# Conformer convolution, sample block, last layer norm and the hand-over of the second half of the tokens, in a four-layer decoder trunk

## The reference, cut to what matters

```python
hp = xp * (1 + sc1p) + sh1p                       # the same for the samples, per sample sequence
op = gmlp_mixer | conv_module | mla (hp)
xp = layer_norm(ALPHA * xp + g1p * op, ln_mix_g[i], ln_mix_b[i])
fp = swiglu_ffn(xp * (1 + sc2p) + sh2p, ffn_w_gate[i], ffn_w_up[i], ffn_w_down[i])
xp = layer_norm(ALPHA * xp + g2p * fp, ln_ffn_g[i], ln_ffn_b[i])

def conv_module(h, ctx, ...):
    a = h @ w_pw1 + b_pw1
    a = a[..., :D_MODEL] * jax.nn.sigmoid(a[..., D_MODEL:])
    full = jnp.concatenate([ctx, a], 1)
    y = depthwise(full, w_dw) + b_dw              # 31 taps along the tokens
    y = jax.nn.silu(layer_norm(y, ln_g, ln_b))
    return y @ w_pw2 + b_pw2, full[:, -(CONV_WIDTH - 1):]

# gmlp_mixer:  z = gelu(h @ w_in);  u, v = halves of z;  v = layer_norm(v);  y = (u * spatial(v)) @ w_out
```

## Time and profile before

| what | before |
|---|---|
| median of 3 executions | 3214.94 us (3214.44 to 3221.95) |
| the profiled execution's own time | 3222.54 us |
| its span, first to last instruction | 3220.3 us |
| PE busy | 3064.5 us, 95% |
| DVE, POOL, ACT busy | 46%, 47%, 17% |
| mean granted clock of PE | 0.983 |

### The profile page before, as it was taken

How to read it: one execution, slowest core, us unless ns; L and a number is a source line. 1 busy time by engine, 2 the same in 40 slices (tenths; PEclk the granted TensorE clock), 3 DMA queues, 4 the chain that set the end, 5 groups by cost and what they waited for, 6 DMA issues and landing times.

```text
span 3220.3 us, 54527 instructions
## 1 busy us (share of the span) xinstructions
PE 3064.5 (95%) x22828; PEld 2858.6 (89%) x22828; DVE 1485.7 (46%) x2487; ACT 543.7 (17%) x1114; POOL 1523.6 (47%) x904
## 2 busy tenths in 40 slices
PE   6999999999999799999999799999999999899997
PEld 5999989999876789999885488999989999899997
DVE  3254653324653753423656445342462535634346
ACT  3121130000220230000224103000022211400002
POOL 2355455545468445545420135554544464555551
PEclk8999999999999899999999999999999999999998
DMA  6542443443243243443222324333322322222221
GB/s 230 216 116 81 121 165 123 131 131 119 82 123 95 81 163 122 132 132 118 75 62 58 107 86 166 123 131 131 119 60 74 104 83 77 78 81 85 83 83 50
DMA packets 455970, 353.86 MB, mean 110 GB/s; under 512 B 26041, under 2 KB 437041, under 8 KB 443422
## 3 DMA queue, kind: packets, MB, share of 16 engines
q1 hardware_dynamic: 441232, 323.74, 31.8%
q10 hardware_dynamic: 14493, 26.63, 2.8%
HBM read 336.81 MB, written 5.25 MB: 106 GB/s over the span
## 4 chain that ended last, share of the span: by engine, by line
PE 81%; DVE 9%; ACT 3%; DVEq 2%; SPq 1%; issue 1%; DMA 1%; ACTq 1%; POOL 1%; POOLq 0%
PE pb L826 80%; DVE h_lo L2107 1%; ACT hf L1590 1%; DVEq L2055 1%; ACT h_hi L1590 1%; DVE pb L2073 1%; DVE part L2054 1%; DMA ada_first<-in_ada_w 1%; DVE xa L2080 1%; DVEq L2079 0%; DVE a_lo L1921 0%; SPq L700 0%; SPq L704 0%; SPq L702 0%; PE pb L921 0%
## 5 line engine op out<-in xcount | busy, mean ns | idle before, releaser
L733 POOL TENSOR_SCALAR w_hi<-w_raw 128x1024 fp32r<-128x1024 f32 (+2 forms) x416 | 448.5, 1078 | 1382.2 <-DMA w_raw<-in_ffn_w_up 400.8
L736 POOL TENSOR_TENSOR w_lo<-w_raw,w_hi 128x1024 fp32r<-128x1024 f32 (+2 forms) x416 | 986.3, 2371 | 69.0 <-issue 69.0
L826 PE MATMUL pb<-h_hi,w_hi 128*128 128x288 f32 x3584 | 975.6, 297 | 22.4 <-DVE h_lo L2107 15.9
L826 PE MATMUL pb<-h_lo,w_hi 128*128 128x288 f32 x3584 | 969.5, 296 | 0.0
L826 PEld LDWEIGHTS pb<-h_hi,w_hi 128*128 128x128 f32 x3584 | 676.1, 189 | 34.5 <-DVE h_lo L2107 21.5
L826 PEld LDWEIGHTS pb<-h_lo,w_hi 128*128 128x128 f32 x3584 | 676.9, 189 | 0.3
L826 PE MATMUL pb<-a_hi,w_hi 128*128 128x288 f32 x2176 | 594.1, 298 | 24.5 <-DVEq L2401 13.1
L826 PE MATMUL pb<-a_lo,w_hi 128*128 128x288 f32 x2176 | 588.6, 295 | 0.0
L826 PE MATMUL pb<-h_hi,w_lo 128*128 128x288 f32 x3584 | 556.4, 295 | 0.0
L826 PEld LDWEIGHTS pb<-h_hi,w_lo 128*128 128x128 f32 x3584 | 504.5, 188 | 0.0
L826 PEld LDWEIGHTS pb<-a_hi,w_hi 128*128 128x128 f32 x2176 | 409.7, 188 | 32.6 <-DVEq L2401 13.5
(11 more groups left out here) (283 smaller groups left out, 2729.5 us busy)
## 6 DMA issues: line engine op xcount, KB each, us to landing
ada_w<-in_ada_w SPq DMA_DIRECT2D x88, 1024.0 KB, 8.0
w_raw<-in_ffn_w_gate SPq DMA_DIRECT2D x88, 512.0 KB, 3.8
w_raw<-in_ffn_w_up SPq DMA_DIRECT2D x88, 512.0 KB, 3.7
w_raw<-in_gmlp_w_in SPq DMA_DIRECT2D x64, 512.0 KB, 4.4
w_raw<-in_ffn_w_down SPq DMA_DIRECT2D x64, 512.0 KB, 3.6
w_raw<-in_gmlp_w_out SPq DMA_DIRECT2D x32, 512.0 KB, 4.4
w_raw<-in_ffn_w_down SPq DMA_DIRECT2D x32, 384.0 KB, 3.3
w_raw<-in_conv_w_pw SPq DMA_DIRECT2D x24, 512.0 KB, 3.8
```

The source lines that it names most:

```text
L733: nc.gpsimd.tensor_scalar(w_hi[:, s, 0:w], w_raw[:, s, 0:w], 1.0, 1.0, ALU.mult, ALU.mult).then_inc(split_hi, 1)
L736: nc.gpsimd.tensor_tensor(w_lo[:, s, 0:w], w_raw[:, s, 0:w], w_hi[:, s, 0:w].bitcast(F32), ALU.subtract).then_inc(split_lo, 1)
L826: return nc.tensor.matmul(out, lhsT, rhs, start=start, stop=stop)
```

## The change

Four parts.

1. **Sample block.** The stationary block of the fifth token tile is `h_both`: 64 columns `h_lo` and 64 columns `h_hi` of the samples, side by side. Both pass under `w_hi` in one matmul and under `w_lo` in another, 16 matmuls for 24. The two parts then lie in different partitions of the bank and are added: ACT copies the lower one to `v_low`, DVE adds it, then comes the Gelu; in MLA, DVE does all of it. DVE builds `h_both` at the beginning of `gmlp` and `mla` (`sample_pairs`), and PE leaves this block to the last part of the second half.
2. **Second half by pairs.** `second_half(p)` hands over two channel tiles; DVE's order is now two `normalise`, `early`, and then per pair: samples, split, next `normalise`. PE takes the second half in four parts. `halves` of the first half stays at four tiles.
3. **Convolution.** The bias `gate * b_pw2` of the prompt goes into `ab`, the shift that ACT adds anyway, and POOL keeps the samples' share alone. `s_sum` and `s_sq` are added up by DVE. POOL makes `diag` for tile m + 1 behind its product for tile m. ACT writes the Silu twice (`hf` and `a_hi`), DVE only subtracts, by pairs, and PE takes the first half of `w_pw2` by pairs. PE transposes the states before the taps' weights.
4. **Last norm.** The channels of the last residual are transposed first, between the last products, into token-major tiles `yt`; the moments come from BN_STATS along the row, and gain and bias are added by POOL (`fgb`, loaded by SP) for the lower parts and by DVE for the upper parts. `second_stats`, the partition sums and the last `normalise` are gone for this norm; eight output transfers take the place of five.

```diff
+def token_parts(hi, lo, both, t):
+    if t == TT - 1:
+        return (lambda k: both[:, k, :],)
+    cols = slice(t * P, (t + 1) * P)
+    return lambda k: hi[:, k, cols], lambda k: lo[:, k, cols]
...
@@ pool, conv
                 for m in range(KT):
                     split_to(plan.mark[l, min(m + 2, KT - 1)])
                     if m == 0:
                         pool.wait_ge(w4_in, 16 * QT)
-                    if m >= 2:
-                        pool.wait_ge(taps_done, m - 1)
...
+                        diagonals(0)
                     pool.wait_ge(full_ready, m + 1)
...
-                    if m:
-                        pool.wait_ge(ysq_ready, m)
-                        pool.drain()
-                        for acc, y in ((s_sum, yc[:, m - 1, :]), (s_sq, sqy[:, (m - 1) % 2, :])):
-                            last = nc.gpsimd.tensor_tensor(acc[:], acc[:], y, ALU.add)
-                        last.then_inc(q_done, 1)
+                    if m + 1 < KT:
+                        if m:
+                            pool.wait_ge(taps_done, m)
+                        diagonals(m + 1)
                     if m == 3:
                         pool.wait_ge(xa_ready, 16 * (2 * l + 1))
...
-                        for k in range(KT):
-                            nc.gpsimd.tensor_scalar(xa[:, k, 0:SEQ], xa[:, k, 0:SEQ], gbw[:, k, 0:1], None, ALU.add)
...
@@ pe, first_four
-                for part_ in range(2):
-                    pe.wait_ge(h_ready, 4 * t + 2 * h + part_ + 1)
+                parts = 4 if h else 2
+                kn = KT // parts
+                for part_ in range(parts):
+                    if h and part_ % 2 == 0:
+                        pe.wait_ge(h_pair, 2 * t + part_ // 2 + 1)
+                    else:
+                        pe.wait_ge(h_ready, 4 * t + 2 * h + (part_ // 2 if h else part_) + 1)
...
@@ act, gmlp_v
+                if tt == TT - 1:
+                    fn(v_low[NS:], pb[0:NS, G.n % BANKS, 0:256], ACT.Copy).then_inc(low_copied, 1)
+                    act.wait_ge(low_added, LA.up())
...
@@ act, conv
+                act.wait_ge(bias_ready, 1)
                 residuals(2 * l)
...
+                        for dst in (hf[:, g, i, :], a_hi[:, m, half_cols(h)]):
+                            last = fn(dst, yc[:, m, half_cols(h)], ACT.Silu,
...
@@ dve, down_norm
+                second.normalise(0, 2)
+                second.normalise(2, 4)
+                early()
+                for p in range(4):
+                    samples(t, p)
+                    second_half(p)
+                    if p < 2:
+                        second.normalise(2 * p + 4, 2 * p + 6)
...
@@ dve, conv, taps
+                    if m:
+                        dve.wait_ge(ysq_ready, m)
+                        for acc, y in ((s_sum, yc[:, m - 1, :]), (s_sq, sqy[:, (m - 1) % 2, :])):
+                            last_ = v.tensor_tensor(acc[:], acc[:], y, ALU.add)
+                        last_.then_inc(q_done, 1)
...
@@ dve, conv, the end
+                def lower(h, p):
+                    ms = slice(2 * p, 2 * p + 2)
+                    dve.wait_ge(hfc_ready, 4 * h + p + 1)
+                    v.tensor_tensor(a_lo[:, ms, half_cols(h)], hf[:, p // 2, 2 * (p % 2):2 * (p % 2) + 2],
+                                    a_hi[:, ms, half_cols(h)].bitcast(F32), ALU.subtract)
+                    dve.drain().then_inc(a_ready, 2)
+
+                def pairs(stats, h):
+                    for p in range(4):
+                        stats.normalise(2 * p, 2 * p + 2, yc, yn_ready)
+                        if p:
+                            lower(h, p - 1)
+                    lower(h, 3)
...
@@ pool, behind the last split
+            for n, (tt, cols) in enumerate(((0, slice(0, D)), (1, slice(0, D)), (2, slice(0, 512)), (3, slice(0, 512)))):
+                pool.wait_ge(xh_ready, n + 1)
+                nc.gpsimd.tensor_tensor(yt[:, tt, cols], yt[:, tt, cols], fgb[:, 0, cols], ALU.mult)
+                pool.drain()
+                nc.gpsimd.tensor_tensor(yt[:, tt, cols], yt[:, tt, cols], fgb[:, 1, cols], ALU.add
+                                        ).then_inc(y_pool, 1)
```

446 lines of the change are left out of this document (297 added, 149 removed).

## The result

| | before | after |
|---|---|---|
| median of 4 executions | 3218.03 us (3214.44 to 3221.95) | 3181.90 us (3179.18 to 3183.53) |
| the profiled execution, its span | 3222.54 us, 3220.3 | 3183.53 us, 3181.7 |
| ratio, 95% interval | | 0.9884 (0.9871 to 0.9897) |
| mean granted clock of PE | 0.983 | 0.985 |

The change makes the kernel 36.1 us faster by the medians and 39.0 between the profiled executions. Forecast were 46.4 us and 3168.5 us: the direction is right and the time lies in the range, but the gain is 10.3 us too large (7.8 between the traces); 3.1 us more come from the median of before, which a fourth execution moved from 3214.94 to 3218.03.

The account below looks back on a forecast made before the run. PE, busy 95% of the span, was taken as the bound: its matmuls and its waits count. Terms 14.4 + 0.3 + 13.0 + 0 - 2.5 + 8.4 + 12.8 = 46.4 us, from 3214.9 to 3168.5 us; range 3153 to 3187.

Parts of the forecast that it names:

- first two rivals: Lock in the convolution and at the end: 3180 us, chance 0.13; waits move but the clock stays: 3178 us, chance 0.15.
- Part 1: Sample block, layers 0 and 3: eight fewer matmuls in each column group, 15 x 0.96 = 14.4 us less.
- Part 2: Sample block in MLA: between 0 and 1.9 us less, taken as 0.3 because PE waits behind it for DVE.
- Parts 3 and 4: Second half by pairs: 13.0 us less at t = 1, 2, 3, 5, 7; 0 at t = 4; -2.5 at t = 6.
- Part 5: Convolution: 6.4 + 3.0 + 1.4 - 2.4 = 8.4 us less.
- (a): Convolution: POOL's bias work goes, with PE's 3.03 us wait for w_hi and a 3.4 us slow stretch: 6.4 us less.
- (b): Convolution: diag of the last tile no longer waits for ACT's square and two additions; PE's 3.00 us wait goes.
- (e): Beginning of the convolution: DVE makes the bias first, and PE's short wait for transposes stays; no gain or loss charged.
- (c): Two norms at the convolution's end: a_lo and Silu by pairs, no cast, ACT writes twice; 1.4 us less.
- (d): Convolution: DVE takes 14 additions, four of them in the last two tiles held 0.6 us each by POOL's splits: -2.4.
- The first rival: Convolution and end: six DVE operations each wait a whole POOL operation of 2.4 us, 14 us; time 3180, chance 0.13.
- Part 6: Last norm: 31.2 us behind the last product become 18.4, with POOL the longest chain: 12.8 us less.

Follow-up runs that it names:

- e12: Changed kernel with the sample block of layers 0 and 3 made of three products again (24 matmuls, no h_both there): 3195.14 us.
- e9: Changed kernel with the second half at t = 0 alone handed over by four channel tiles, t = 1 to 7 still by pairs: 3181.11 us.
- e6: Changed kernel with the second half handed over by four channel tiles again at all eight inputs, no pairs: 3191.24 us.
- e1: Changed kernel with DVE making the convolution's bias behind its eight copies of the states instead of ahead of them: 3179.84 us.
- e8: Changed kernel with the convolution's bias made behind the first two tiles of full, and ACT's residual behind its third set of x4 transfers: 3180.49 us.
- e3: Changed kernel with POOL starting its five splits of w_pw2 only when the last yc is written, DVE's operations unchanged: 3177.57 us.
- e10: Changed kernel with DVE, in the last norm, inverting the deviations of token tiles 0 and 1 before adding product (6, second half): 3181.68 us.

## Why the forecast was right in direction, and where it was wrong

The range held the time, but 3181.90 us lies 13.4 from the forecast 3168.5 and nearer to the first two rivals, 3180 and 3178. Neither of them is what happened as a whole: the lock cost 5.4 us in the last two tiles and not 14, and the pairs kept most of their gain. The miss is mostly one part, the convolution (-6.6 us); elsewhere errors of both signs cancel.

**Part 1, 14.4 us: right.** e12 gives 13.2. Layer 0 shows only 5.8 of 7.7 us because part 3 takes 1.5 of it back there (e9).

**Part 2, 0.3: right.** PE's wait grew from 3.70 to 5.39 us while 1.92 us of matmuls went, 0.2 us net. No run tests it by itself, and the stretch as a whole holds a slow clock worth 2 us (last section).

**Parts 3 and 4, 10.5: about right in sum (9.3 by e6, 7.8 by its trace), wrong in two terms.** First, the step "t = 1, 2, 3, 5, 7" leaves out t = 0. PE has no wait for `h_lo` pairs there, but behind them the v statistics give its banks back, and the split costs 1.5 us (e9). The sentence that it "costs little here" and "the sum stays" was wrong at this place: the rule of the Trainium skill (VectorE: DVE Perf Modes, "Rules for kernel authors", minimise the number of operations) held where DVE has nothing but that work. Second, the clock. Two stretches of 1.7 us were taken as gone, since the earlier trace rows shows 0.52 behind a wait of 1.82. In e6 the same wait at three places is followed by a clock of 1.00. The slow stretch follows such a wait in some executions only (two of the six places: t = 1 and 3 before, not t = 5 before, none in e6), so 3.4 was an accident of one trace, not a price. At t = 7, where I took 1.1 us of it, the clock is 0.50 after as before. t = 6 cost 2 us less than I had priced, t = 5 brought 1.4 more. That the sum came out near 10.5 is luck in part: these two cover what t = 0 and the clock took.

**Part 5, 8.4 (8.9 with the second wait of t = 2): wrong, 2.3 measured.** Step by step: (a) the bias on POOL, 6.4, and (b) `diag`, 3.0, together 9.4, measured 8.8 between first and last taps. Right, as a sum of two waits that are gone. (e) "PE's short wait for transposes stays" was the failed step: the start lost 3.7 us. PE's wait there was 2.88 us before and is 2.23 + 2.54 after, so that the gated products begin 2.0 us later, and at a clock of 0.55 in their first 6 us (0.87 before) they take 15.3 us for 13.6. e1 takes 2.46 us off these waits by moving the bias alone, and e8 gives 3.1 of the 3.7 us back. I had looked at PE's wait and not at what stood behind DVE's bias operations on DVE: the coefficients and the copies that free PE's banks. (c) and (d), +1.4 and -2.4, came out as -2.8 together. The four additions were counted right and their hold was too small: they cost 3.8 us more than their 3.0 (1.97 + 1.59 + 1.68 + 1.58 - 3.0), where 2.4 was charged, and two small TENSOR_SCALAR operations, which I did not count, 1.6 more. If all 5.4 us reached PE, (c) brought 2.6 and not 1.4; no run tests that. The first rival had the right mechanism at the right place and a wrong size: a DVE operation waits for the rest of POOL's, 0.8 to 1.2 us here, not for a whole one of 2.4.

The rule behind that rival (SBUF — State Buffer, "Who interferes with whom", in the Trainium skill) goes further than I used it: besides instructions with two SBUF inputs it names `copy`, `cast` and `tensor_scalar` as able to take the shared port pair. The trace agrees: L2603 is a TENSOR_SCALAR and lasted 4.29 us beside a POOL operation of 4.20. It also says that `tensor_reduce` never contends on trn2: L2601 took 2.21 us beside the splits and 2.21 without them (e3). Had the whole section been applied, the 1.6 us would have been in the sum.

**Part 6, 12.8 (14.0 behind the last product): right, 14.7 measured.** The transfer at the end took 2.4 us, not 3.3, and POOL started 0.8 us ahead of the last product's end, not 0.5. e10 shows that two other chains stand less than 2 us behind POOL's, which the forecast did not have.

**"What would show it"** held at five of seven points: sample blocks of 16 matmuls, `h_lo` 22.1 us, no wait for `w_hi` or `diag`, a longer bank wait (6.31), a longer wait behind t = 6 (2.64). Two came out shorter. The end took 16.5 us for "about 19" (by the forecast's own terms, -0.5 + 14.4 + 3.3, it should have said 17.2). The wait at the norm was to be near 10 and is 7.7, because PE now comes later to it, through the 4.24 us of new waits in the statistics. A sign of being wrong was seen once, the wait for a bank at 61.07; its cause was part 3's split (e9), not the sample block.

## What to carry to other kernels

When work is moved to an engine that is idle half of the time, look at the engine that left a gap beside it: DVE's additions of 0.75 us cost 1.6 to 2.0 because POOL splits weights at that moment, and moving POOL's work (one wait) was worth 4.8 us. When an operation is put at the head of a queue, follow everything behind it up to the end of the next stage, not only the wait of the engine that one watches (here three bias operations at the head, 1.5 us long there, cost 2.5 us of PE's waits); and splitting a hand-over pays only where the receiver waits for it, so it is decided input by input (here t = 0 lost 1.5 us, t = 5 gained 3.4).
